# Slab order in the front of a decoder step, and the prompt's compression in eight tiles

## What is computed

```python
mod = jax.nn.silu(c) @ w_ada + b_ada                     # (1+8) x 6144
z   = h @ w_in                                           # 288 x 5400
def compress(k, pe, w1, w2):                             # on the cache, and on the prompt's own kc, vc
    chunks = k.reshape(B, n_chunks, 16, G, dh)           # stride 16, block 32
    w1r = w1.reshape(2, 16 * dh, 128)
    pre = pe.reshape(-1) @ w1
    for j in range(2):
        pre = pre + einsum('bngf,fh->bngh', chunks[:, j:j + n_cmp], w1r[j])
    return gelu(pre) @ w2
```

## Time and profile before

| | us |
|---|---|
| median of 3 runs | 1721.73 |
| lowest and highest run | 1720.87, 1728.93 |
| the profiled execution | 1725.74 |
| its span, first to last instruction | 1723.9 |
| front, to the end of w6 | 279.3 |
| TensorE busy, share of the span | 88% |

### The profile page before, as it was taken

How to read it: one execution, slowest core, us unless ns; L and a number is a source line. 1 busy time by engine, 2 the same in 40 slices (tenths; PEclk the granted TensorE clock), 3 DMA queues, 4 the chain that set the end, 5 groups by cost and what they waited for, 6 DMA issues and landing times.

```text
span 1723.9 us, 21845 instructions
## 1 busy us (share of the span) xinstructions
PE 1509.4 (88%) x8284; PEld 669.8 (39%) x8285; DVE 379.5 (22%) x803; ACT 291.9 (17%) x541; POOL 84.8 (5%) x122
## 2 busy tenths in 40 slices
PE   5998989869977955999999998999999899998980
PEld 5544556458854523333333232333332232232220
DVE  6010011346723253111010101010111010010106
ACT  5000013543511010111111101111111111011110
POOL 1000003100000000000000000000000000000002
PEclk9999987978996975999999999999999998999995
DMA  9746764681154632996999999899999999999954
GB/s 277 247 149 230 267 244 117 202 295 42 50 161 137 257 142 100 395 416 267 404 418 417 419 417 419 353 416 418 419 416 419 417 418 419 416 419 417 419 224 158
DMA packets 139315, 527.56 MB, mean 306 GB/s; under 512 B 11554, under 2 KB 40634, under 8 KB 104259
## 3 DMA queue, kind: packets, MB, share of 16 engines
q1 hardware_dynamic: 128482, 482.81, 71.3%
q0 software_dynamic: 10784, 44.07, 7.5%
HBM read 499.85 MB, written 31.15 MB: 308 GB/s over the span
## 4 chain that ended last, share of the span: by engine, by line
PE 58%; DMA 15%; SPq 15%; DVE 8%; issue 3%; ACT 2%; POOL 0%; POOLq 0%; DVEq 0%; ACTq 0%
PE bank L1264 18%; SPq L627 12%; DMA arena<-in_b_up 10%; PE bank L1286 7%; PE bank L1116 4%; PE bank L736 3%; PE bank L941 3%; DMA arena<-in_w_in 3%; PE bank L942 3%; PE bank L1258 2%; PE bank L1189 2%; SPq L632 2%; DMA arena<-in_cache_cmp,arena 1%; PE bank L1177 1%; PE bank L1275 1%
## 5 line engine op out<-in xcount | busy, mean ns | idle before, releaser
L1264 PE MATMUL bank<-arena 128*64 128x512 f32 x2176 | 491.8, 610 | 0.0
L1264 PEld LDWEIGHTS bank<-arena 128*64 128x64 f32 x2176 | 155.3, 140 | 338.3 <-issue 338.3
L1286 PE MATMUL bank<-arena 128*64 128x512 f32 x1088 | 256.0, 625 | 0.0
L2057 DVE TENSOR_SCALAR arena<-bank 128x512 f32<-128x512 f32 x34 | 23.5, 692 | 836.9 <-PE bank L1264 836.9
L1286 PEld LDWEIGHTS bank<-arena 128*64 128x64 f32 x1088 | 77.8, 143 | 154.8 <-issue 154.8
L1572 ACT ACTIVATE arena<-arena 128x512 f32<-128x512 f32 x34 | 21.4, 629 | 524.4 <-DVE arena L2057 524.4
L1234 PE MATMUL bank<-arena 128*64 128x512 f32 (+1 forms) x420 | 103.1, 609 | 8.0 <-DVE arena L2047 8.0
L2134 POOL DMA_DIRECT2D slots<-arena x68 | 36.0, 529 | 1294.3 <-ACT arena L1579 1292.1
L1116 PE MATMUL bank<-arena 128*128 128x288 f32 x256 | 77.2, 453 | 12.9 <-DMA arena<-in_w_in 9.9
L1258 PE MATMUL bank<-arena 1*64 1x512 f32 x272 | 41.6, 683 | 36.8 <-DMA arena<-in_b_up 35.2
L941 PE MATMUL bank<-arena 128*128 128x512 f32 (+1 forms) x112 | 58.4, 604 | 7.3 <-DMA arena<-in_w_in 5.7
(11 more groups left out here) (387 smaller groups left out, 1324.8 us busy)
## 6 DMA issues: line engine op xcount, KB each, us to landing
arena<-in_w_up SPq DMA_DIRECT2D x256, 1024.0 KB, 19.3
arena<-in_w_down SPq DMA_DIRECT2D x128, 1024.0 KB, 22.6
arena<-in_w_ada SPq DMA_DIRECT2D x12, 2048.0 KB, 10.8
slots<-arena POOLq DMA_DIRECT2D x2, 6400.0 KB, 37.0
arena<-in_w_in SPq DMA_DIRECT2D x6, 2048.0 KB, 12.7
slots<-arena POOLq DMA_DIRECT2D x68, 128.0 KB, 5.5
arena<-in_w_in SPq DMA_DIRECT2D x16, 512.0 KB, 3.9
arena<-in_w_out SPq DMA_DIRECT2D x1, 4096.0 KB, 17.4
```

What stands on the lines that cost most here:

```text
L1264: last = mm(banks[part][SLOT * s:SLOT * s + SLOT, :], xcT[:, q], ring[pos][:, D * part + 512 * s:D * part + 512 * s + 512], start=False, s ...
L1286: last = mm(banks[4][SLOT * s:SLOT * s + SLOT, :], lhs, ring[pos][:, D * v + 512 * s:D * v + 512 * s + 512], start=False, stop=f == 7)
```

## The change

The list of slabs becomes a0 to a5, then w0 a6 w1 a7 w2 a8 w3 a9 w4 a10 a11 w5 w6, with a4 and a5 used before `convolve(1)` (`FRONT` = 6). The prompt's own compression takes the 32 columns of `kvTo` as weights and `w1` (128 columns) as the moving side; the two halves of rows (K, V) and four column groups (position modulo 4) make eight tiles, so each of K and V has four partial sums in the four quarters of a bank. ScalarE copies these (`parts`), and two matmuls with a constant 0/1 matrix `stack32` (`own_sums`) add the quarters and turn the result, after w6. Gelu moves behind that, the own keys' copy and the Silu of `hg` behind the first two ring copies, and `own_values` behind two `window_keys` and `importance`.

```diff
+    _put("stack32", (p[:, None] % NS == np.arange(NS)[None, :]) * 1.0)
...
-SLABS = [("a", n) for n in range(4)] + [("w", 0), ("a", 4), ("a", 5), ("w", 1)]
-for _n in range(6, 9):
-    SLABS += [("a", _n), ("w", _n - 4)]
-SLABS += [("a", 9), ("a", 10), ("a", 11), ("w", NZ - 2), ("w", NZ - 1)]
+SLABS = [("a", n) for n in range(6)] + [("w", 0)]
+for _n in range(6, 10):
+    SLABS += [("a", _n), ("w", _n - 5)]
+SLABS += [("a", 10), ("a", 11), ("w", NZ - 2), ("w", NZ - 1)]
+FRONT = 6
...
-            modulation(3)
+            for n in range(3, FRONT):
+                modulation(n)
...
             convolve(1)
             pe.wait_ge(S("gelu"), 4)
+            pe.wait_ge(S("mod_v"), FRONT)
...
                 for s in range(32):
                     for v in range(2):
-                        last = mm(banks[4 + v][:, P:P + 2 * NCMP_P], w1[DH * v:DH * v + DH, s],
-                                  kvTo[DH * v:DH * v + DH, :, s % 16, s // 16:s // 16 + NCMP_P], start=s == 0, stop=s == 31)
+                        half = slice(DH * v, DH * v + DH)
+                        last = mm(banks[4 + v][32 * (s % 4):32 * (s % 4) + 32, 0:P], kvTo[half, 32 * (s % 16) + s // 16:32 * (s % 16) + s // 16 + 32],
+                                  w1[half, s], start=s < 4, stop=s >= 28)
+                last.then_inc(S("own_part"), 1)
+
+            def own_sums():
+
+                after(pe, "own_parts")
+                for v in range(2):
+                    last = mm(banks[4 + v][:, 256:256 + NS], parts[:, v], C("stack32"), start=True, stop=True)
                 last.then_inc(S("own_pre"), 1)
...
-            own_values()
+            own_sums()
             for b in range(2):
                 window_keys(b)
             importance()
+            own_values()
             probs_T("cmp", 0, 1)
...
-                    after(act, "own_pre")
+                    after(act, "own_part")
                     for v in range(2):
-                        fn(geTo[:, v, :, 0:NCMP_P], banks[4 + v][:, P:P + 2 * NCMP_P].rearrange("p (g c) -> p g c", g=G),
-                           ACT.Gelu_apprx_tanh, bias=pconst[:, v:v + 1]).then_inc(S("gelu"), 1)
-
-            after(act, "own_comp")
-            nc.scalar.copy(kcT[:, NB * NCMP:NC_ALL], banks[4][:, 160:160 + NCMP_P]).then_inc(S("own_a"), 1)
-            in_place("hg", 512, ACT.Silu, NZ)
+                        last = nc.scalar.copy(parts[:, v], banks[4 + v][:, 0:P])
+                    last.then_inc(S("own_parts"), 1)
+
+            after(act, "own_pre")
+            for v in range(2):
+                fn(geTo[:, v], banks[4 + v][:, 256:256 + NS].rearrange("p (g c) -> p g c", g=G),
+                   ACT.Gelu_apprx_tanh, bias=pconst[:, v:v + 1]).then_inc(S("gelu"), 1)
...
             for b in range(2):
                 keys_out("win", b, 0)
+            after(act, "own_comp")
+            nc.scalar.copy(kcT[:, NB * NCMP:NC_ALL], banks[4][:, 160:160 + NCMP_P]).then_inc(S("own_a"), 1)
+            in_place("hg", 512, ACT.Silu, NZ)
             probs_out("cmp", 0, 0)
```

More of the change, by code:

```diff
@@ L118 @@
 STEPS = {
-    "pe_step": ('idx_ps', 'sct_ps', 'peT_ps', 'prow_ps', 'pconst_ps', 'modT_ps', 'comp_ps', 'sq_ps', 'own_ps', 'score_ps', 'own_pre', 'own_comp', 'imp_ps', 'lg_ps', 'cnt_ps', 'base_ps'),
-    "act_step": ('silu_c', 'comp_a', 'sg_gate', 'hf_sig', 'own_a', 'lb', 'gl', 'gate_sig', 'all_out'),
+    "pe_step": ('idx_ps', 'sct_ps', 'peT_ps', 'prow_ps', 'pconst_ps', 'modT_ps', 'comp_ps', 'sq_ps', 'own_ps', 'score_ps', 'own_part', 'own_pre', 'imp_ps', 'own_comp', 'lg_ps', 'cnt_ps', 'base_ps'),
+    "act_step": ('silu_c', 'comp_a', 'sg_gate', 'hf_sig', 'own_parts', 'own_a', 'lb', 'gl', 'gate_sig', 'all_out'),
     "dve_step": ('zeroed', 'zero_t', 'pt_f', 'idx', 'sct', 'peT', 'prow', 'pconst', 'comp_v', 'affine', 'sq', 'own_T', 'imp', 'own_v', 'mod_w', 'lb_d', 'f', 'hk', 'vm', 's_free', 's_kq', 'onS', 'nch', 'tab'),
 }
-SLABS = [("a", n) for n in range(4)] + [("w", 0), ("a", 4), ("a", 5), ("w", 1)]
-for _n in range(6, 9):
-    SLABS += [("a", _n), ("w", _n - 4)]
-SLABS += [("a", 9), ("a", 10), ("a", 11), ("w", NZ - 2), ("w", NZ - 1)]
+SLABS = [("a", n) for n in range(6)] + [("w", 0)]
[3 more added lines that the diff above has]
+FRONT = 6
 RING = ([("win", 0), ("win", 1), ("cmp", 0)] + [("win", b) for b in range(2, NB)] + [("sel", n) for n in range(6)]
@@ L290, in build @@
         zero_t = take(P)
-        take(NB * NPG)
+        take(NB * NPG - NS)
         pt8 = take(NB).bitcast(I32)
@@ L350, in build @@
         geT = view(raw_at, 4 * 520, 2, 2, 520)
-        kvTo = view(raw_at + 4 * 520, 2 * 16 * 16, 2, 16, 16)
+        kvTo = view(raw_at + 4 * 520 - 8, 2 * 16 * 16 + 8)
         gates_at = n_t + 3 * ZW
@@ L362, in build @@
         geTo = view(pTs_at + 8 * 256, 64, 2, 2, 16)
+        parts = view(pTs_at + 7 * 256, 2 * P, 2, P)
         sSc = view(pTs_at + 9 * 256, 128, 2, 64)
@@ L741, in modulation @@
                 n = SLABS[i][1]
-                bank = banks[4 + n % 2] if n < 4 else banks[7 * (n % 2)]
+                bank = banks[4 + n % 2] if n < FRONT else banks[7 * (n % 2)]
                 pe.wait_ge(S(f"ld_slab{slab_at(i)}"), 16 * slab_use(i))
@@ L916, in _ @@
             after(pe, "comp_v")
-            for i in range(4, len(SLABS)):
+            for i in range(FRONT, len(SLABS)):
                 what, n = SLABS[i]
@@ L1626, in _ @@
                     normed_rows(b)
-            for n in range(4):
+            for n in range(FRONT):
                 if n == 3:
@@ L1635, in _ @@
                 dve.wait_ge(S("slab_used"), n + 1)
-                V.tensor_copy(mod0[:, n], banks[4 + n % 2][:, 0:P]).then_inc(S("mod_v"), 1)
+                if n < 4:
+                    V.tensor_copy(mod0[:, n], banks[4 + n % 2][:, 0:P]).then_inc(S("mod_v"), 1)
+                else:
+                    dve.wait_ge(S("ld_bada"), 64)
+                    V.tensor_tensor(mod[:, n - 4], banks[4 + n % 2][:, 0:P], bada[:, n - 4], ALU.add).then_inc(S("mod_v"), 1)
             after(dve, "modT_ps")
@@ L1658, in sample_inputs @@
                 V.memset(imp, 0.0)
+                V.memset(kvTo[:, 512:], 0.0)
                 link(dve, "dve", V.memset(qz, 0.0))
@@ L1670, in sample_inputs @@
                     for g in range(G):
-                        last = V.tensor_copy(kvTo[DH * v:DH * v + DH, g],
+                        last = V.tensor_copy(kvTo[DH * v:DH * v + DH, 0:512].rearrange("p (s g c) -> p g s c", g=G, c=16)[:, g],
                                              banks[7][DH * g:DH * g + DH, 256 * v:256 * v + 256].rearrange("p (c s) -> p s c", s=16))
@@ L1701, in compressed_softmax @@
                 V.tensor_tensor(imp3[:, :, 0:14], imp3[:, :, 0:14], sSc[:, :, 3:56:4], ALU.add).then_inc(S("imp"), 1)
-                after(dve, "own_pre")
+                after(dve, "own_part")
                 for g in range(G):
@@ L1708, in compressed_softmax @@
                 last.then_inc(S("probs"), 1)
-            dve.wait_ge(S("ld_bada"), 64)
-            for i in range(4, len(SLABS)):
+            for i in range(FRONT, len(SLABS)):
                 what, n = SLABS[i]
```

## The result

The changed kernel takes 1714.07 us (median of 6 runs, 1710.64 to 1717.43) against 1726.03 for the kernel before in 6 runs (1720.87 to 1729.42), ratio 0.9933, interval 0.9909 to 0.9957. By medians that is 12.0 us less, by the ratio 11.6. The forecast was 12.0 less. The interval leaves out 1: the gain is real, 0.4 to 0.9%. In a later session the same kernel took 1713.71 (1709.62 to 1714.74), ratio 0.9937 (0.9914 to 0.9960).

The account below looks back on a forecast made before the run. TensorE, busy 88%, bounds it. Front +8.2, w0 to w4 -9.9 + 3.0, w4 to w5 -5.7, clock +7.2, own compression -10.1, w6 -2.8, tail -1.9: -12.0, so 1709.7 us against the median of 1721.7; range 1701 to 1719.

Parts of the forecast that it names:

- one to one to the end: Behind the front: what is won or lost at the start of the selected keys (298.6) carries fully to the end.
- Front, +8.2 and the clock: Ahead of the second convolution: a4 and a5 there start it at 100.9 instead of 92.66, plus 8.2; clock charged separately.
- w2: At slab w2, queued behind the 3 MB window state: a new wait of 3.0 us (2.0 to 4.5).
- w4 to w5: From w4's end to w5's start: 9.2 us instead of 14.9, minus 5.7, with 0.3 us for overlapping gathers.
- Clock after the waits: After the three new waits (3.6, 3.0, 4.3 us): lower clock costing 2.4 us each, plus 7.2 (0 to 9.3).
- Rival (a): At the new waits: too short to bring the clock down, or only one does; 1702.5 to 1705 us, chance 0.2.
- rival (d): At the waits: each 2 us longer, and the tail gives nothing; 6 to 9 us lost, 1716 to 1720, chance 0.13.
- Own compression: The prompt's own compression in eight tiles: 2.5 us, minus 10.1; 5.0 (up to 7.4) at half clock.
- Rival (c): In the own compression: eight tiles don't overlap; at half clock 29.7 us, 30.0 more in all, 1739.7; chance 0.05.
- w6: Slab w6, behind the own compression: full clock, 9.6 us instead of 12.47, minus 2.8 (zero the other end).
- Rival (b): Around the own compression: clock falls, compression takes 5 to 7.4 us, w6 keeps its 2.8; 1715 to 1717.5, chance 0.22.
- Tail: After w6, up to the selected keys: first ring copies 2.6 us behind w6; minus 1.9 us (0 to 2.6).

## Why the prediction was right, step by step

The forecast was 12.0 us less, and 12.0 came by medians. The mechanism holds: every wait stood where it was forecast, with its releaser, and the own compression, w6 and the tail gave what they should within 1.3 us each. That the number fits to the tenth is luck: the interval spans 7.4 to 15.7 us, and in the trace the stages gave 2.1 us more than the sum in one profile and 3.5 in the other, with errors of both signs in them.

**What bounds it, and one to one to the end.** Right in the main, not for a single profile, and open by 2 to 3 us (see above): the part behind the selected keys varies by 8 us between executions, two thirds of the forecast's size. By the sign that I had set, the first profile won 13.0 us by the selected keys (298.58 to 285.63) and kept 8.2 to the end; the second won 13.3 and kept 14.0. What showed the change is the front's distance, -14.1 and -15.5 in its two profiles.

**Front, +8.2 and the clock.** +10.4 against 10.6. a5 landed 17.05 us after 82.97, where I had 16.5 from its issue, and 0.6 us later behind a3 than forecast. Its own wait was 3.46 in the second profile and 2.11 in the first, where a4's wait and gap took the rest: the sum is set by a5's landing, whatever stands before.

**w2.** Forecast 3.0, measured 3.02 and 2.73; removing the state from ahead of it removed it.

**w4 to w5.** -6.1 against -5.7, waits of 4.00 and 3.69 against 4.3. w5 landed 8.48 us after its issue (8.35 for w1 in the earlier trace rows) with the gathers beginning beside it, and in the other kernels with a wait at w5 between 8.2 and 9.0. The spread is as large as the terms in question, so the trace can't tell my 0.3 us from none or from the 0.7 to 1 that I had worked out for even sharing. The rule behind that estimate, that DMAs of all queues run on the same 16 engines and interleave, is the Trainium skill's (Trainium Kernel Development and Optimization, Key Constraints); no run here tests it.

**Clock after the waits.** I charged three times 2.4, 7.2. Measured in the first profile: a5's slab 3.3 (100.07 to 103.36) instead of 1.9, 1.4 (the other 0.8 by which the front exceeds 8.2 are a5's later landing and the transposes); w2's slab 17.25 (175.82 to 193.07) instead of 15.7, 1.5; w5 1.6 over its 17.41: 4.6 in all. This is the term that was too large, by 2.6. Rival (a), no drop or only one, did not come: the first instruction behind each wait shows the lower clock. Nor did rival (d): no wait came out 2 us longer, and the tail gave more than it had. The size per wait isn't fixed: behind a wait of about 3 us at w2 the same slab cost 0.0 (seven slabs in front), 1.5 and 1.7 (the change), and 3.1 (slab order alone, 173.26 to 192.05). Behind a wait of 3.45 at a5 the kernel with the own compression twice lost nothing.

**Own compression.** 3.34 against 2.5, both within my bounds of 1.7 to 3.7. The price of the tiles was right and even a little high (2.02 without gaps); what I missed are gaps without a releaser. Rival (c), tiles that don't overlap, falls with it. The rule of the Trainium skill (TensorE: Matmul & The Clock Gate, Part 1), starts never closer than about 25 ns, would have given 3.2 and so looks right in the first profile; the 128 records in 2.02 us, 16 ns each, show that it doesn't hold for tiles beside each other. The time agreed with the rule for another reason.

**w6.** -2.3 against -2.8; it runs at full clock. Rival (b), a compression of 5 to 7.4 us with w6 slow behind it, came in none of the twelve profiles with the new form. A milder case came in three of the twelve, but in neither of the change itself: 105 records in 2.8 to 3.2 us instead of 1.78, and 1 to 2 us lost in all.

**Tail.** -3.2 against -1.9, outside my own bounds of 0 to 2.6. The waits were right: ScalarE starts the ring copies 2.5 us behind w6 (272.08, forecast 2.6) and `probs_T` starts 3.3 behind it (272.81, forecast 3.2), minus 1.3. What I had too small is the clock: I put 1.3 us on the half clock of before and took half of it; the granted clock stayed at 1.00 through the whole tail (from 269.55), which gave the other 1.9. Undoing it cost 3.7 in time.

**What the sum hid.** By my own terms the slab order was a loss of about 2.8 us (8.2 - 9.9 + 3.0 - 5.7 + 7.2) and everything gained lay in the own compression, w6 and tail (14.8). I added them up and did not say so. The order alone measured 0.9994, the other half alone 0.9929: the second half of the change carries all of it. And the waits that the sum priced at 8.2 + 3.0 + 4.3 and clock were the larger thing to win: taking them out gave another 16 us. Of the signs that I named, two were missed narrowly: the second convolution started at 104.15 instead of by 104, and w6 took 10.13 us instead of under 10.

## What to carry to other kernels

Look up when a load can be issued (which use frees its buffer) and what stands ahead of it in its queue before moving its use: moving a use ahead of its landing only moves the wait, and a large load of another kind one place earlier or later in the list decides whether the next slab is there. Put work whose data arrive late behind a long stage, not ahead of it; here the same two slabs cost 7 us less on the other side of the convolution. Price a change as separate halves and say which half pays.

## What the runs showed of the hardware that I had not expected

64 x 32 tiles with 128 columns moving ran at 16 ns a record (128 in 2.02 us, eight tiles), nearly twice as fast as 128 x 32 tiles (29 ns a record, 64 in 1.85 us). 64 matmuls with 128 weight columns and 30 moving ones started at full clock (35 records in 2.0 us) and fell to a granted clock of 0.50 with no wait within them. Long runs of such short instructions met gaps of 0.3 to 2.6 us with no releaser, longer with gathers running beside them in the one pair compared. Waits of nearly the same length (2.7 to 3.1 us, at w2) were followed by a slab that cost nothing more or up to 3.1 us more. The same code behind the selected keys took 1424.6 to 1432.8 us.
